# The second SwiGLU network in seven half-block products

## The chip, the cores and the metric

One core of one Trainium2 chip runs the kernel. The metric is the time of one execution on the device, in microseconds.

## What is computed

One layer of a decoder, on 1024 tokens and 16 learned ones ahead of them, in float32: a half-weighted SwiGLU network, two attentions mixed by gates, a second half-weighted SwiGLU network. The case is about the last one:

```python
def swiglu_ffn(u, w_gu, w_down):
    g, up = jnp.split(u @ w_gu, 2, axis=-1)
    return (jax.nn.silu(g) * up) @ w_down
...
        h = h + 0.5 * swiglu_ffn(rms_norm(h, ffn2_norm[l]), ffn2_w_gu[l], ffn2_w_down[l])
    return h[:, N_META:]
```

D_MODEL is 1024, D_FF is 2816; w_gu is 1024 x 5632, w_down 2816 x 1024.

## The kernel before

Tensors lie in blocks of 128 partitions: the model's width is KD = 8 blocks, the hidden width FT = 22. h stays on the chip, transposed (width on the partitions, tokens along the free axis). Every float32 product is made of three matmuls of fp32r operands (mm3, L71 to L75: high by high, low by high, high by low). ScalarE makes the high part (a cast), and VectorE or GpSimd the low part (the subtraction of the high part). So each 128 x 1024 block of weights that SP loads into `raw` costs ScalarE one cast (L387) and GpSimd one subtraction (L445).

ffn_phase computes both networks. For the second the tokens go in two chunks of 512 (REAL_TOKENS). It first normalizes: TensorE adds up the squares over the partitions (L199), ScalarE takes the root (L219), VectorE the reciprocal (L245), TensorE broadcasts it (L208), VectorE scales h (L252), and the two parts of u are made. Then there are 11 groups of two hidden blocks. gate_up multiplies the gate and up weights of a block with u, ScalarE applies silu (L411), VectorE multiplies (L523) and splits the hidden block (L526, L528); down multiplies the group before with its down weights, and VectorE adds half of each result to h (L539). The loops of TensorE, VectorE, ScalarE, GpSimd and SP over the groups are hardware loops (Fori). Each engine works through its own list in order, and waits on semaphores; SP issues every transfer in the order of its list, also one that waits for nothing, behind those that wait. The last group is followed by Store: TensorE transposes h back (L299), ScalarE and VectorE copy the rows (L312), and SP stores them (L319). The output projection (out_proj_phase) runs just before the second network; it is written out, without a loop.

## Time and profile before

| | us |
|---|---|
| median of 3 runs | 2772.76 |
| lowest and highest | 2771.84, 2775.6 |
| span of the profiled execution, first to last instruction | 2767.1 |
| first matmul of the second network's gate | 2033.05 |
| first transpose behind its last matmul | 2755.83 |

The profiled execution has no time of its own beside the span; the median of the runs lies 5.7 us above it. Busy time is the time in which an engine worked on an instruction. The columns behind the bar in a group give the idle time just before its instructions and what ended most of it. The granted clock is the share of TensorE's full speed (2.4 GHz) that it was given; 0.5 is 1.2 GHz.

### The profile page before, as it was taken

The numbers are of one execution on the slowest core, as the hardware profiler recorded it, in microseconds if no ns is written. First come the engines' busy times: TensorE is split into PE (matmuls) and PEld (weight loads), VectorE is DVE, ScalarE is ACT, GpSimd is POOL, SyncE is SP. The second block draws the span as 40 slices with busy tenths as digits, with TensorE's granted clock in tenths as the row PEclk, the third lists the DMA queues.
The fourth block names the chain that finished last, engine by engine and source line by source line (L and its number), as shares of the span: only waits on it lengthen the run. The fifth ranks groups of instructions, "written<-read, shape, count | busy, mean of one in ns | idle before, by whom it ended". The sixth has DMA issues, their size and how long they took to land. (4 is left out here: it accounts for less than half of the span.)

```text
span 2767.1 us, 37228 instructions
## 1 busy us (share of the span) xinstructions
PE 2600.7 (94%) x13802; PEld 2307.1 (83%) x13802; DVE 1106.3 (40%) x1994; ACT 682.5 (25%) x1285; POOL 749.7 (27%) x711
## 2 busy tenths in 40 slices
PE   7999999999978999988999979997979999999999
PEld 6999999999968888876787768886868888888887
DVE  5233332333375566533766651112143333333324
ACT  4111111111044445432444441112131111111101
POOL 4222222222122333221444462222142222222210
PEclk8999999999989999987988999999989999999999
DMA  3211111111011000000000011112021111111101
GB/s 127 67 47 46 47 46 47 46 47 46 8 76 47 25 24 0 1 31 9 4 7 4 3 39 61 45 38 92 31 68 61 46 58 49 45 45 45 51 33 61
DMA packets 32510, 116.05 MB, mean 42 GB/s; under 512 B 4016, under 2 KB 5936, under 8 KB 32256
## 3 DMA queue, kind: packets, MB, share of 16 engines
q1 hardware_dynamic: 32384, 114.29, 12.3%
q8 instruction: 89, 1.46, 0.2%
q14 instruction: 37, 0.30, 0.0%
HBM read 105.49 MB, written 8.65 MB: 41 GB/s over the span
## 5 line engine op out<-in xcount | busy, mean ns | idle before, releaser
L73 PE MATMUL f_bank<-u_hi,f_w_hi 128*128 128x384 f32 (+2 forms) x1760 | 612.5, 348 | 16.6 <-POOL u_lo L232 13.3
L445 POOL TENSOR_TENSOR f_w_lo<-f_raw,f_w_hi 128x1024 fp32r<-128x1024 f32 x132 | 328.2, 2507 | 1101.9 <-ACT f_w_hi L387 1101.9
L74 PE MATMUL f_bank<-u_hi,f_w_lo 128*128 128x384 f32 (+2 forms) x1760 | 611.9, 348 | 0.0
L75 PE MATMUL f_bank<-u_lo,f_w_hi 128*128 128x384 f32 (+2 forms) x1760 | 611.8, 348 | 0.0
L523 DVE TENSOR_TENSOR f_work<-f_work,f_bank 128x384 f32<-128x384 f32 (+2 forms) x110 | 64.3, 584 | 781.2 <-PE f_bank L75 771.0
L73 PEld LDWEIGHTS f_bank<-u_hi,f_w_hi 128*128 128x128 f32 x1760 | 332.3, 189 | 45.9 <-issue 18.3
L75 PEld LDWEIGHTS f_bank<-u_lo,f_w_hi 128*128 128x128 f32 x1760 | 332.1, 189 | 27.6
L74 PEld LDWEIGHTS f_bank<-u_hi,f_w_lo 128*128 128x128 f32 x1760 | 332.2, 189 | 27.5
L75 PE MATMUL f_bank<-f_hid_lo,f_w_hi 128*128 128x384 f32 (+2 forms) x880 | 306.3, 348 | 0.0
L74 PE MATMUL f_bank<-f_hid_hi,f_w_lo 128*128 128x384 f32 (+2 forms) x880 | 306.0, 348 | 0.0
L73 PE MATMUL f_bank<-f_hid_hi,f_w_hi 128*128 128x384 f32 (+2 forms) x880 | 305.7, 347 | 0.0
L387 ACT CAST f_w_hi<-f_raw 128x1024 fp32r<-128x1024 f32 x132 | 132.4, 1050 | 548.7 <-PE f_bank L75 537.7
L411 ACT ACTIVATE f_work<-f_bank 128x384 f32<-128x384 f32 (+2 forms) x110 | 56.6, 516 | 625.2 <-PE f_bank L75 625.2
L73 PEld LDWEIGHTS f_bank<-f_hid_hi,f_w_hi 128*128 128x128 f32 x880 | 165.8, 188 | 13.6
L75 PEld LDWEIGHTS f_bank<-f_hid_lo,f_w_hi 128*128 128x128 f32 x880 | 165.2, 188 | 13.7
L74 PEld LDWEIGHTS f_bank<-f_hid_hi,f_w_lo 128*128 128x128 f32 x880 | 165.2, 188 | 13.6
L539 DVE SCALAR_TENSOR_TENSOR h_in<-f_bank,h_in 128x384 f32<-128x384 f32 (+1 forms) x264 | 135.7, 518 | 98.6 <-PE f_bank L75 98.4
L539 DVE SCALAR_TENSOR_TENSOR h_out<-f_bank,h_out 128x512 f32<-128x512 f32 x176 | 119.1, 689 | 90.2 <-PE f_bank L75 90.2
L1510 POOL TENSOR_TENSOR mla_p_lo<-mla_p,mla_p_hi 128x512 fp32r<-128x512 f32 (+4 forms) x112 | 106.4, 950 | 67.7 <-DVE mla_p_hi L1861 67.5
L73 PE MATMUL fox_bank<-u_hi,fox_w_hi 128*128 128x384 f32 (+1 forms) x288 | 98.3, 341 | 16.5 <-DVE fox_w_lo L1267 16.5
L528 DVE TENSOR_TENSOR f_hid_lo<-f_work,f_hid_hi 128x384 fp32r<-128x384 f32 (+2 forms) x110 | 109.0, 991 | 3.8
L73 PE MATMUL gt_bank<-u_hi,gt_w_hi 128*128 128x512 f32 x256 | 100.7, 393 | 9.6 <-POOL gt_w_lo L1920 9.6
(277 smaller groups left out, 4287.1 us busy)
## 6 DMA issues: line engine op xcount, KB each, us to landing
f_raw<-in_ffn SPq DMA_DIRECT2D x132, 512.0 KB, 3.8
gt_raw<-in_gate SPq DMA_DIRECT2D x24, 512.0 KB, 3.7
fox_raw<-in_fox SPq DMA_DIRECT2D x12, 512.0 KB, 4.4
kept_hsave<-h_in SPq DMA_DIRECT2D x1, 4160.0 KB, 12.7
h_out<-kept_hsave SPq DMA_DIRECT2D x8, 520.0 KB, 6.3
ld_xin<-in_x SPq DMA_DIRECT2D x8, 512.0 KB, 4.5
op_raw<-in_wout SPq DMA_DIRECT2D x8, 512.0 KB, 5.4
out<-f_raw SPq DMA_DIRECT2D x6, 512.0 KB, 4.1
```

Source lines behind the costliest of these rows:

```text
L73: nc.tensor.matmul(out, w_hi, x_hi, start=first, stop=False)
L74: nc.tensor.matmul(out, w_lo, x_hi, start=False, stop=False)
L75: return nc.tensor.matmul(out, w_hi, x_lo, start=False, stop=last)
L387: nc.scalar.copy(w_hi[:, slot, :], raw[:, n_rem, :]).then_inc(whi_done, 1)
L411: nc.scalar.activation(silu[:, u % 2, 0:n], bank[2 * (u % 2)][:, 0:n], ACT.Silu).then_inc(silu_done, 1)
L445: nc.gpsimd.tensor_tensor(w_lo[:, slot, :], raw[:, raw_slot, :], w_hi[:, slot, :].bitcast(F32), ALU.subtract).then_inc(wlo_done, 1)
L523: nc.vector.tensor_tensor(h32[:, 0:n], silu[:, u % 2, 0:n], bank[2 * (u % 2) + 1][:, 0:n], ALU.mult).then_inc(h32_done, 1)
L528: nc.vector.tensor_tensor(hid_lo[:, parity, f, columns(t0, n)], h32[:, 0:n], hid_hi[:, parity, f, columns(t0, n)].bitcast(F32), ALU.subtra ...
L539: nc.vector.scalar_tensor_tensor(g.h[:, d, t0:t0 + n], bank[4 + v % 4][:, 0:n], 0.5, g.h[:, d, t0:t0 + n], ALU.mult, ALU.add).then_inc(dow ...
L1510: nc.gpsimd.tensor_tensor(p_lo[:, w % 2, 0:n], p32[:, w % 2, 0:n], p_hi[:, w % 2, 0:n].bitcast(F32), ALU.subtract).then_inc(plo_done, 1)
```

## The change

The first network keeps its code, under the name plain_ffn_phase. The second gets a new ffn_phase, written out without loops, with W = 512 tokens in each half.

It uses Strassen's form (Winograd's variant of it). Both large products are cut in two along tokens, inner width and outer width: seven products of half blocks stand for eight. For gate and up a group p (FP = 11 of them) is 2 gate and 2 up blocks, and each is cut into two halves of the inner width; 7 steps j = 0 to 6 each multiply a sum of weight quarters with a sum of input quarters (4 blocks of inner width, 2 halves x of output blocks: 24 matmuls of 512 columns). The results are added up in four pairs of PSUM banks where the form allows it; ScalarE copies intermediate sums out (snap), VectorE the last ones (evacuate). The seven sums of u (split into both parts) stay on the chip in u_hi, u_lo and two new tensors. For that, u's quarters are computed in place of h, which SP saves to DRAM first (save) and brings back later (reload). VectorE makes the four sums of weights per group (weight_mix) and all low parts (weight_lo, u_lo). GpSimd makes only the four sums of the down weights, which SP loads (load_down) and stores to DRAM in blocks of 128 columns, 512 bytes (store_down). The hidden blocks and their sums go to DRAM too (store_hidden, store_first, store_mixed).

Only after all 77 steps come the down products: 28 units n (7 products jj x 4 output blocks), each 11 x 3 matmuls; load_s brings the unit's weights (704 KB), load_t the hidden pieces (512 KB), ScalarE and VectorE split them (s_hi, s_lo, t_hi, t_lo), add_down adds to h. The transposes, copies and stores of the output lie among the last 12 units. The host rearranges the weights accordingly. The diff, cut:

```diff
-def ffn_phase(nc, g, tag, d_blocks, gain_col, chunks, first=False):
+def plain_ffn_phase(nc, g, tag, d_blocks, gain_col, chunks, first=False):
...
+FP = FT // 2
+STEPS = 7 * FP
+UNITS = 28
+SUM_OF = {1: (1, 2), 2: (None, 0), 3: (3, None), 4: (0, 1)}
+RAW_OF = {0: 0, 5: 3, 6: 2}
+TARGET = ((4, 1), (0, 1), (0, 0), (0, 0), (0, 1), (4, 1), (4, 0))
...
+def ffn_phase(nc, g, tag, d, gain_col, tb, W, first=False):
...
+        T1, T2, T3, T4 = [hf[:, n * W:(n + 1) * W] for n in range(4)]
+        WD = [hf[:, 4 * W + 512 * k:4 * W + 512 * k + 512] for k in range(4)]
...
+        def t_raw(z):
+            x = piece(z % 6)
+            return rw[:, 4 * D + (z % 3) * 2 * W:4 * D + (z % 3) * 2 * W + x.stop - x.start]
...
+        @block.sync
+        def _(sp):
+            def load(m):
+                sp.dma_start(raw_block(m), d["gu"][m // 4, m % 4]).then_inc(raw_in[m % 5], 16)
+            def save(i, kh, th):
...
+                sp.dma_start(d["keep"][x], g.h[x]).then_inc(h_saved[i], 16)
...
+            def store_first(p):
+                sp.wait_ge(t_done, 4 * p + 1)
+                sp.dma_start(d["hid"][0, :, p, :], T1).then_inc(t1_stored, 16)
...
+            def store_mixed(p):
+                sp.wait_ge(t_done, 4 * p + 4)
+                sp.dma_start(d["hid"][4:7, :, p, :].rearrange("j p w -> p j w"),
...
+            def load_down(i):
+                if i == 0:
+                    sp.wait_ge(blo_done, 14)
+                else:
+                    sp.wait_ge(s_stored, 64 * i)
+                sp.dma_start(hf[:, 4 * W:4 * W + 4 * 512], d["wd"][i]).then_inc(wd_in, 16)
+            def store_down(i):
+                sp.wait_ge(s_added, 4 * i + 4)
+                for k in range(4):
+                    sp.dma_start(d["dsum"][k, :, :, i * P:(i + 1) * P].rearrange("a p b -> p a b"),
+                                 WD[k].rearrange("p (a b) -> p a b", a=4)).then_inc(s_stored, 16)
+            def load_t(z):
+                jj, q = z // 6, z % 6
+                if z >= 3:
+                    sp.wait_ge(tlo_done, z - 2)
+                src = d["hid"][jj].rearrange("p a b -> p (a b)")[:, piece(q)]
+                sp.dma_start(t_raw(z), src).then_inc(rt_in[z % 3], 16)
...
+            def load_s(n):
+                if n >= 2:
+                    sp.wait_ge(slo_done, n - 1)
+                sp.dma_start(s_raw(n), s_source(n)).then_inc(rs_in[n % 2], 16)
+            def reload(i, tiles):
+                x = (slice(None), tiles, slice(tb, tb + 2 * W))
+                sp.dma_start(g.h[x], d["keep"][x]).then_inc(h_back[i], 16)
...
+            load(0)
+            save(0, 0, 0)
+            load(1)
+            load(2)
+            save(1, 0, 1)
+            save(2, 1, 1)
+            load(3)
+            load(4)
+            save(3, 1, 0)
+            for p in range(FP):
+                if p:
+                    store_hidden(p - 1)
+                    load_down(p - 1)
+                if p + 1 < FP:
+                    sp.wait_ge(add_done, 4 * p + 4)
+                    load(4 * p + 5)
+                    load(4 * p + 6)
+                if p:
+                    store_first(p - 1)
+                    store_mixed(p - 1)
+                    store_down(p - 1)
+                if p + 2 < FP:
+                    sp.wait_ge(wlo_done, 7 * p + 6)
+                    load(4 * p + 8)
+                if p + 1 < FP:
+                    sp.wait_ge(wlo_done, 7 * p + 7)
+                    load(4 * p + 7)
+            load_down(FP - 1)
+            sp.wait_ge(wlo_done, STEPS - 2)
+            sp.wait_ge(t1_stored, 16 * (FP - 1))
+            for z in range(3):
+                load_t(z)
+            store_down(FP - 1)
+            sp.wait_ge(b_stored[(FP - 2) % 2], 48 * (FP // 2))
+            sp.wait_ge(t_done, 4 * (FP - 1))
+            reload(0, slice(4, KD))
+            sp.wait_ge(add_done, 4 * FP)
+            sp.wait_ge(s_stored, 64 * FP)
+            load_s(0)
+            sp.wait_ge(wlo_done, STEPS)
+            load_s(1)
+            reload(1, slice(2, 4))
+            for z in range(3, 5):
+                load_t(z)
+            store_first(FP - 1)
+            sp.wait_ge(t1_stored, 16 * FP)
+            load_t(5)
+            store_hidden(FP - 1)
+            store_mixed(FP - 1)
+            sp.wait_ge(t_stored, 16 * FP)
...
+            for n in range(UNITS):
...
+                if n + 2 < UNITS:
+                    load_s(n + 2)
+                if jj < 6:
+                    for q in PIECES_OF[dp]:
+                        load_t(6 * (jj + 1) + q)
+                if not first and n >= 20:
...
+        @block.gpsimd
+        def _(pool):
+            for i in range(FP):
+                pool.wait_ge(wd_in, 16 * (i + 1))
+                nc.gpsimd.tensor_tensor(WD[3], WD[2], WD[3], ALU.add).then_inc(s_added, 1)
...
+            def t_hi(z):
+                jj, q = z // 6, z % 6
+                if z == 0:
...
+                nc.scalar.copy(t_buf(near_hi, far_hi, jj)[:, piece(q)], t_raw(z)).then_inc(thi_done, 1)
+            def s_hi(n):
+                if n >= UNITS:
+                    return
+                if n == 0:
+                    act.wait_ge(prod_done, 2 * (STEPS - 3))
...
+                act.wait_ge(rs_in[n % 2], 16 * (n // 2 + 1))
+                nc.scalar.copy(s_buf(near_hi, w_hi, n), s_raw(n)).then_inc(shi_done, 1)
...
+            for st in range(3, STEPS):
+                snap(st - 1, 1)
+                silu(st - 1, 1)
+                weight_hi(st + 2)
+                if st == STEPS - 3:
+                    t_hi(0)
+                    t_hi(1)
+                elif st == STEPS - 2:
+                    t_hi(2)
+                    t_hi(3)
+                elif st == STEPS - 1:
+                    t_hi(4)
+                    s_hi(0)
...
+            def product(st, x):
+                p, j = st // 7, st % 7
+                out = ps[(0, 2, 0, 2, 0, 2, 0)[j] + x]
+                if x == 0:
+                    pe.wait_ge(wlo_done, st + 1)
+                if j == 0 and p:
...
+                elif j == 6:
+                    pe.wait_ge(up_done, 2 * p + 1 + x)
...
+                for k in range(4):
+                    if p == 0 and x == 0 and k % 2 == 0:
+                        pe.wait_ge(blo_done, 2 * j + k // 2 + 1)
...
+                    for i, (w, u) in enumerate(((wh, uh), (wl, uh), (wh, ul))):
+                        for b in range(NS):
+                            last = nc.tensor.matmul(out[:, b, 0:N], w[:, c], u[:, b * N:(b + 1) * N],
+                                                    start=(j in (0, 1, 5) and k == 0 and i == 0),
+                                                    stop=(k == 3 and i == 2), skip_group_check=True)
+                last.then_inc(prod_done, 1)
+            def down(n):
...
+                pe.wait_ge(slo_done, n + 1)
+                if n < 2:
+                    pe.wait_ge(hid_done, 4 * FP - 1 + n)
...
+                for k in range(FP):
+                    if dp == 0 and k % 2 == 0:
+                        pe.wait_ge(tlo_done, 6 * jj + k // 2 + 1)
...
+            def evacuate(st, x):
+                p, j = st // 7, st % 7
...
+                dve.wait_ge(prod_done, 2 * st + x + 1)
+                if j == 3:
...
+                    nc.vector.tensor_tensor(parts(e2(p, x)), acc(2 + x), parts(e2(p, x)), ALU.add).then_inc(gate_done, 1)
+                elif j == 4:
+                    dve.wait_ge(snapped, 6 * p + 3 + x)
+                    nc.vector.tensor_tensor(parts(e5(p, x)), acc(x), parts(e5(p, x)), ALU.add).then_inc(up_done, 1)
+                    dve.wait_ge(up_done, 2 * p + 1 + x)
+                    dve.wait_ge(silu_done, 4 * p + 1 + x)
...
+            def first_sum(p):
+                dve.wait_ge(hid_done, 4 * p + 3)
...
+                nc.vector.tensor_tensor(T1, e2(p, 0), e1(p, 0), ALU.subtract).then_inc(t_done, 1)
...
+            def more_sums(p):
+                dve.wait_ge(hid_done, 4 * p + 4)
...
+            def t_lo(z):
+                jj, q = z // 6, z % 6
+                dve.wait_ge(thi_done, z + 1)
+                nc.vector.tensor_tensor(t_buf(near_lo, far_lo, jj)[:, piece(q)], t_raw(z),
...
+            def s_lo(n):
...
+                dve.wait_ge(shi_done, n + 1)
+                nc.vector.tensor_tensor(s_buf(near_lo, w_lo, n), s_raw(n), s_buf(near_hi, w_hi, n).bitcast(F32),
+                                        ALU.subtract).then_inc(slo_done, 1)
...
+            dve.wait_ge(rooted, 2 if first else 1)
+            if first:
+                nc.vector.reciprocal(rstd[0:META, 0:1], rstd[0:META, 0:1])
+            nc.vector.reciprocal(rstd[:, 1:QT + 1], rstd[:, 1:QT + 1]).then_inc(inverted, 1)
+            weight_lo(0)
+            scaled(0, 0)
+            u_lo(0, 0)
+            u_lo(0, 1)
+            weight_mix(1)
+            scaled(0, 1)
+            mix_first(0)
+            mix_first(1)
+            weight_lo(1)
+            scaled(1, 1)
+            u_lo(1, 0)
+            u_lo(1, 1)
+            mix_second(0)
+            mix_second(1)
+            weight_mix(2)
+            mix_third(0)
+            mix_third(1)
+            u_lo(2, 0)
+            u_lo(2, 1)
+            weight_lo(2)
+            weight_mix(3)
+            u_lo(3, 0)
+            u_lo(3, 1)
+            weight_lo(3)
+            weight_mix(4)
+            u_lo(4, 0)
+            u_lo(4, 1)
+            scaled(1, 0)
+            u_lo(5, 0)
+            u_lo(5, 1)
+            mix_fourth(0)
+            mix_fourth(1)
+            weight_lo(4)
...
+            for st in range(3, STEPS):
+                p, j = st // 7, st % 7
+                evacuate(st - 1, 1)
+                weight_lo(st + 2)
+                weight_mix(st + 3)
+                if p and j == 2:
+                    first_sum(p - 1)
+                if p and j == 3:
+                    more_sums(p - 1)
+                if st == STEPS - 3:
+                    t_lo(0)
+                    t_lo(1)
+                elif st == STEPS - 2:
+                    t_lo(2)
+                    t_lo(3)
+                elif st == STEPS - 1:
+                    t_lo(4)
+                    s_lo(0)
+                evacuate(st, 0)
+            first_sum(FP - 1)
+            evacuate(STEPS - 1, 1)
+            s_lo(1)
+            more_sums(FP - 1)
+            t_lo(5)
+            for n in range(UNITS):
+                add_down(n - 1)
...
@@ -2179,7 +2969,7 @@
             hb = placed(nc, stream, "")
             g.h, g.sumsq = hb("h_out", [P, KD, T]), hb("sumsq_out", [P, T])
             out_proj_phase(nc, g)
-            ffn_phase(nc, g, "f2", g.dram["ffn2"], g.FFN2_GAIN, REAL_TOKENS)
```

SUM_OF, RAW_OF, QUARTER_OF and TARGET say which sums a step takes and where a result is added. slot(w, st) gives three weight slots in turn; snap and silu on ScalarE follow TensorE by half a step. T1 to T4 and WD lie in the room of h. Before the loop of ScalarE stand weight_hi(0), the root, the copies of the broadcast, u_hi and weight_hi(1) to weight_hi(4), in the order of VectorE's list above.

## Rows read from the trace of the kernel before

**Rows 1.** The page: span, then busy time of each engine, its share and instructions.

```profile
span 2767.1 us, 37228 instructions
...
PE 2600.7 (94%) x13802; PEld 2307.1 (83%) x13802; DVE 1106.3 (40%) x1994; ACT 682.5 (25%) x1285; POOL 749.7 (27%) x711
```

**Rows 2.** Busy us (instructions) by stretch, engines as headed, then clock, DMA share, GB/s.

```profile
core 0: us, PE busy (x) PEld busy (x) DVE busy (x) ACT busy (x) POOL busy (x), PEclk, DMA share, GB/s
1925.00:1950.00 25.00, 25.00 (x112) 20.69 (x111) 2.85 (x5) 4.03 (x4) 5.46 (x3) 1.00 0.40 141
...
2033.00:2037.20 4.20, 4.16 (x10) 3.33 (x11) 4.20 (x5) 1.42 (x4) 3.97 (x2) 0.53 0.19 42
2045.00:2100.00 55.00, 55.00 (x244) 45.58 (x243) 13.57 (x15) 8.90 (x11) 17.35 (x7) 1.00 0.24 77
...
2600.00:2700.00 100.00, 100.00 (x443) 82.83 (x442) 28.09 (x38) 12.21 (x15) 19.91 (x8) 1.00 0.11 37
```

**Rows 3.** Groups by shape after 2000 us: busy, mean ns, idle before, releaser.

```profile
L73 PE MATMUL f_bank<-u_hi,f_w_hi 128*128 128x512 f32 x704 | 274.7, 390 | 8.0 <-POOL u_lo L232 8.0
...
L539 DVE SCALAR_TENSOR_TENSOR h_out<-f_bank,h_out 128x512 f32<-128x512 f32 x176 | 119.1, 689 | 90.2 <-PE f_bank L75 90.2
L528 DVE TENSOR_TENSOR f_hid_lo<-f_work,f_hid_hi 128x512 fp32r<-128x512 f32 x44 | 74.6, 1697 | 1.5
L387 ACT CAST f_w_hi<-f_raw 128x1024 fp32r<-128x1024 f32 x66 | 66.2, 1052 | 280.3 <-PE f_bank L75 276.0 <-DMA f_raw<-in_ffn 4.3
...
L411 ACT ACTIVATE f_work<-f_bank 128x512 f32<-128x512 f32 x44 | 26.3, 598 | 294.0 <-PE f_bank L75 294.0
```

**Rows 4.** In order of time, second network's start: start, us, engine, line.

```profile
2017.07 1.28 SPq L363 DMA_DIRECT2D f_raw<-in_ffn  x3
2017.09 1.28 ACT L219 ACT_TABLE_LOAD   x1 [1.79 <-PEq L2049]
...
2017.13 3.55 PE L199 MATMUL f_bank<-ones,sumsq_out 128*128 128x1 f32 x16 [7.50 <-PEq L2049]
2020.71 0.27 ACT L219 ACTIVATE f_norm_rstd<-f_bank,gains 128x8 f32<-128x8 f32 x1 [2.34 <-PE f_bank L199]
...
2021.27 3.78 PE L208 MATMUL f_bank<-ident,f_norm_rstd 128*128 128x128 f32 x16 [0.60 <-DVE f_norm_rstd L245]
...
2033.05 0.76 PE L73 MATMUL f_bank<-u_hi,f_w_hi 128*128 128x512 f32 x1 [7.99 <-POOL u_lo L232]
```

**Rows 5.** In order of time at the end, TensorE.

```profile
2755.83 4.82 PE L299 MATMUL f_bank<-ident,h_out 128*128 128x128 f32 x40
```

**Rows 6.** Groups by shape over the whole span, VectorE: busy us, mean ns.

```profile
L1267 DVE TENSOR_TENSOR fox_w_lo<-fox_raw,fox_w_hi 128x512 fp32r<-128x512 f32 x24 | 16.1, 682 | 4.3 <-ACT fox_w_hi L1003 4.3
...
L252 DVE SCALAR_TENSOR_TENSOR f_work<-h_out,gains,f_bank 128x512 f32<-128x512 f32 x16 | 11.2, 741 | 2.2 <-PE f_bank L208 2.2
...
L2035 DVE TENSOR_TENSOR gt_o_lo<-o_mla,gt_o_hi 128x1024 fp32r<-128x1024 f32 x2 | 6.8, 3417 | 0.0
...
L821 DVE TENSOR_TENSOR lt_w_lo<-lt_raw,lt_w_hi 128x1024 fp32r<-128x1024 f32 x1 | 1.2, 1226 | 6.1 <-ACT lt_w_hi L799 6.1
```

**Rows 7.** The same groups, GpSimd.

```profile
L993 POOL TENSOR_TENSOR fox_p_lo<-fox_p,fox_p_hi 128x512 fp32r<-128x512 f32 x36 | 46.4, 1294 | 39.7 <-DVE fox_p_hi L1351 39.7
```

**Rows 8.** DMA issues over the span: KB each, median us to landing.

```profile
f_raw<-in_ffn SPq DMA_DIRECT2D x132, 512.0 KB, 3.8
...
kept_hsave<-h_in SPq DMA_DIRECT2D x1, 4160.0 KB, 12.7
...
mla_w_head<-in_mla SPq DMA_DIRECT2D x8, 192.0 KB, 2.4
...
ident<-in_ident SPq DMA_DIRECT2D x1, 64.0 KB, 1.8
```

**Rows 9.** GB/s in 40 equal slices of the stretch 1905 to 1960 us.

```profile
GB/s 0 0 0 0 0 0 45 370 407 407 398 425 388 378 367 354 352 380 311 30 0 0 0 0 244 428 97 0 0 12 0 12 277 404 76 0 0 0 0 0
```

**Rows 10.** In order of time at the end, VectorE.

```profile
2760.69 0.69 DVE L312 COPY f_raw<-f_bank 128x512 f32<-128x512 f32 x1 [0.18 <-PE f_bank L299]
```

488 lines of the change are left out of this document (484 added, 4 removed).

## The prediction

> **What bounds the kernel now.** I read the page first. TensorE is busy 94% of the 2767.1 us span; VectorE has 40%, ScalarE 25%, GpSimd 27% [rows 1]. The chain of work that ended last also lies on TensorE. The windows then say how evenly it runs: in the second network (from 2033 us) TensorE has no idle time, the granted clock is 1.00 (the 2.4 GHz level), and 443 matmuls start in 100 us, 226 ns each [rows 2]. The groups by shape confirm the cover: VectorE waits 90.2 us for TensorE before the additions at L539 and ScalarE 276.0 us before L387, never the other way round except for 8.0 us at the start (L73 waits for u_lo) [rows 3]. So a matmul taken away is worth its 226 ns, as long as what prepares and empties it keeps up.
>
> **What the change takes away.** Gate, up and down are 44 x 8 + 22 x 8 = 528 blocks of 128 x 128 weights, each times two token chunks and three split terms: 3168 matmuls of 512 columns. Their phase begins at 2033.05 [rows 4] and ends at 2755.83 [rows 5]. Ten of them ran at clock 0.53 (the 1.2 GHz level) in 4.2 us [rows 2], 1.9 us more than at 226 ns; 24 transposes of 4.82/40 = 0.12 us, 2.8 us, lie among them. That leaves (2755.83 - 2033.05 - 1.9 - 2.8)/3168 = 0.2267 us each. After the change there are 77 steps x 2 x 4 x 3 = 1848 and 28 units x 11 x 3 = 924, in all 2772, again of 512 columns: 628.4 us, where 718.2 were. The 396 matmuls are worth **89.8 us**. A step is then 5.44 us and a down unit 7.48 us. That all of it is unrolled costs nothing: the unrolled output projection also starts 112 matmuls in 25 us, beside 141 GB/s [rows 2].
>
> **Steady steps.** Per seven steps (38.1 us) VectorE has 11 operations of 1024 elements at 1.226 us and 14 of 512 at about 0.69 [rows 3, 6]: 23.1 us. ScalarE has 7 x 1.05 + 10 x 0.6 = 13.4 us [rows 3]. GpSimd adds 4 x 1.3 us [rows 7]. All fit. The tightest hand-over is the last product of a group of seven to the first of the next, through one pair of banks: 0.69 us of emptying against 2.7 us of the other half's product. GpSimd can lengthen it: a subtraction beside a GpSimd one took 1.70 us (L528) [rows 3] where 0.68 us is the time alone (L1267) [rows 6]; two engines alternating made 1.2 us into 3.4 (L2035) [rows 6]. Even 4 x 1.3 us added gives 28.3 of 38.1 us, so I take nothing, with 2.6 us per group as the other end. SBUF — State Buffer in the Trainium skill (Who interferes with whom) says that the second of the two engines blocks fully until the first is done; the rows agree, and by that rule the worst case is the 2.6 us, which the rival below prices.
>
> **Start, +17.1 us.** Before, TensorE starts 12 us after the broadcast begins and then never waits. Now VectorE alone prepares seven sums of the input. ScalarE splits a weight block before it takes the root: a load takes 3.8 us to land [rows 8], so the root comes at 2017.07 + 3.8 + 1.05 + 1.28 (a table load, L219 [rows 4]) = 2023.2 instead of 2020.7; then 0.3 + 0.3 + 2.1 for the first broadcast + 0.6 for its copy: the first scaling at 2026.4. The stored copy of h has landed by then (1.5 MB at some 390 GB/s [rows 9] and 2 us of landing: 2024). From there to the fifth step VectorE has 16 scalings of 0.70 (0.69 of L539 and 0.74 of L252 [rows 3, 6]), 12 low parts, 8 mixes of the input, 4 mixes and 4 low parts of weights: 11.2 + 28 x 1.226 = 45.5 us. TensorE can't do step 5 before 2071.9; it has done four steps (21.8 us) by then, so it is as if it had started at 2050.1. After each gap the clock falls; the last one costs about 2 us more, as above: 2052.1, against 2033.05 + 1.9 = 2035.0. First matmul near 2030.5, gaps of some 5, 4 and 6 us before steps 2, 3 and 5. Bounds: 11 us if the root isn't delayed and the hand-overs cost nothing, 24 us if each of some 40 hand-overs costs 0.15 us more.
>
> **From products to down units, +38.3 us.** This is what the order of SP's queue makes. Let t = 0 be the start of step 73 (j = 3 of the last group). The three sums of group 9 end at 1.7 (ScalarE's split) + 1.2 + 2.1 = 5.0. Behind them SP stores 0.79 MB and the four mixed down blocks, 1.05 MB in pieces of 512 bytes. Saturated transfers run at 354 to 428 GB/s [rows 9] (I take 390) and a landing costs some 2 us besides (512 KB 3.8, 4160 KB 12.7 [rows 8]). The trace has no such store. By bytes it takes 2.7 us. If nothing of the 128 pieces in the identity matrix's 1.8 us overlapped [rows 8], its 2048 pieces would take 29. 64 KB and 192 KB, each 128 pieces, differ by 0.6 us [rows 8], so the bytes count and the pieces little; I take 4.5 us, near the low end. s_stored comes at 5.4 + 2.0 + 4.5 + 2 = 14. Only then SP loads the last down weights (4.7 us, 18.7) and, behind them, the first three hidden pieces, the first at about 20. But VectorE stands at t_lo(0), in step 74, and behind that at evacuate(74, 0), for which product 76 waits: it starts at about 24 instead of 16.3. Next GpSimd adds until 24, the store and a 2.1 MB reload of h occupy the queue until 34.5, load_s(0), load_s(1), 1.05 MB and load_t(3) follow: 3.7 + 2.7 + 1.3, landing at 44.2. VectorE stands at t_lo(3) before evacuate(75, 0). From there t_hi and t_lo 2.3, two evacuations 1.4, t_lo(4) about 3 with ScalarE's silus and splits, s_lo(0) 1.9, evacuate(76, 0) 0.7: down(0) starts at 53.5. Without stalls it would start at 4 x 5.44 = 21.8: **31.8 us**. Then load_s(2) queues behind store_mixed(10) and reload(2): its s_lo is ready 20 us after down(0) starts, two units need 15: 5 us. The clock after these gaps 1.5 us. Bounds: 28 us (store by bytes alone, nothing lost in hand-overs) to 50 us.
> DMA: Bandwidth & Descriptors in the Trainium skill (Specifications) puts line rate at pieces of 512 bytes or more. No row here shows it. By it the store takes 2.7 us and this term is 3.6 us smaller, about 2735 us in the end.
>
> **Down units.** In 7.48 us VectorE has 1.7 + 1.8 + 0.7 + 0.7 = 4.9 us and the queue moves 1.5 MB, 200 GB/s of 390; a load is asked for two units ahead. Nothing.
>
> **End.** Now 40 transposes, a copy and a store stand behind the last matmul: 2767.1 - 2755.8 = 11.3 us [rows 5, 10]. After: addition 0.8, 4 transposes 0.5, two copies 1.4, the last store of 256 KB 4.8: 7.5 us. The other 56 transposes lie among the units, 6.7 us.
>
> **The sum.** 2052.1 + 628.4 + 38.3 + 6.7 + 7.5 = 2733.0 of span against 2767.1: 34.1 us less. The median of the runs shown is 2772.8, 5.7 us above the span (launch and end around it), and I keep that: **2739 us**. The working's own bounds are -6 and +7 at the start and -10 and +12 in the middle; combined, 2722 to 2757.
>
> **Rivals.** First, the middle is covered better than I read it (the loads land before VectorE reaches them, or the stores drain in time): 30 us come back, 2709 us. For it: only the order of instructions, not their durations, says that VectorE stands still. Against: s_stored stands in front of the loads in the text of the change, and the sums that feed it end only in step 73. Chance 0.08.
> Second, GpSimd's additions fall on the tight hand-over in each group: 2.6 us x 11 = 29 us, 2767 us. For: the 1.70 and 3.4 us above. Against: the additions start early in a group, when there is slack. Chance 0.12.
> Third, slower than before: the stores in 512-byte pieces clog the queue in every group. The last load of a group is asked behind them; it lands at 28.7 us + s of a group, and VectorE needs it at about 41. From s = 12.3 us each further us costs 10 us over the groups, besides 2 in the middle: at s = 14 the gain is gone, at s = 20 it is +77 + 31 - 34 = 74 us, 2847 us. For: the 29 us bound. Against: the small difference of the two loads above. Chance 0.08.
> That the products aren't fewer can't be: the loops give 2772.
>
> **The numbers.** Forecast 2739 us, 0.72; the rivals 0.08, 0.12, 0.08. The range leaves out the first and the third and reaches to the second: 2716 to 2766. A measurement here can tell about 0.2%, 5.5 us: faster than 2767.2 has nearly all of the forecast, the first rival and a little under half of the second, 0.85; within 0.2% 0.06; slower 0.09.
>
> **What would show it.** 2772 matmuls of 512 columns at 0.227 us and clock 1.00 in the steady part; VectorE without pause before step 5; idle TensorE in three gaps at the start; then 8 us before product 76 and some 24 before down(0), VectorE idle before t_lo(0), t_lo(3) and s_lo(0) with a DMA as releaser; the store of mixed down blocks landing in about 6.5 us; under 1 us of idle TensorE per group between. I am wrong if TensorE idles in every group, if that store takes over 12 us, or if the two transitions together cost under 40 or over 75 us.

## The result, and the profile after

The changed kernel takes **2738.6 us** (median of 4 runs, 2737.0 to 2754.1) beside 2772.3 us for the kernel before on the same chip: a ratio of 0.9895, interval 0.9864 to 0.9925. It is 1.1% faster, and the forecast was 2739 us. A second measurement of the same file, the first experiment below, gives 0.9852 (0.9808 to 0.9895). The forecast was right in the time; several of its terms were off, with opposite signs.

The page of the kernel after, span and busy times (the lines that answer to [rows 1]):

```profile
span 2735.2 us, 36205 instructions
...
PE 2530.9 (93%) x13406; PEld 2242.9 (82%) x13406; DVE 1257.3 (46%) x2073; ACT 812.9 (30%) x1432; POOL 651.9 (24%) x681
```

TensorE's share has fallen from 94% to 93% although it is busy 69.8 us less: it waits now in places where it didn't. To compare only what the change touches, I measure each trace from SP's first load of the second network to the end of the span and call that **the stretch**. Before it is 2767.1 - 2017.07 = 750.0 us [rows 1, 4]; after it is 2735.2 - 2023.10 = 712.1 us. The prediction's terms, added up without what lies ahead, make 715.9. Steps are counted from 1 where the text speaks of the start, as the prediction does, and from 0 in names such as product 76 and down(0).

First, the groups that answer to [rows 3], after 2000 us (busy us, mean ns | idle before, releaser):

```profile
L1020 PE MATMUL f_ps<-u_hi,f_w_hi 128*128 128x512 f32 x352 | 140.9, 400 | 9.9 <-DVE u_lo L1117 6.7 <-DVE f_w_lo L1180 2.8
...
L1020 PE MATMUL f_ps<-f_far_hi,f_w_hi 128*128 128x512 f32 x264 | 104.3, 395 | 11.2 <-DVE f_ev L1193 7.2 <-DVE f_w_lo L1180 4.0
...
L1043 PE MATMUL f_ps<-u_hi,f_w_hi 128*128 128x512 f32 x110 | 43.3, 394 | 1.2 <-DVE f_w_lo L1234 1.2
...
L1043 PE MATMUL f_ps<-u_hi 128*128 128x512 f32 x66 | 27.3, 414 | 20.6 <-DVE u_lo L1234 20.6
```

Line 1020 is the seven products, line 1043 the down units. The idle time ahead of them is most of what the change gives back: 13.5 us of waiting for VectorE's low parts at the start (6.7 + 2.8 + 4.0), 7.2 us for an emptied bank at L1193, 20.6 us for the first hidden pieces of the down units and 1.2 us for the weights of the third unit. Second, three windows (columns as in [rows 2]): the steady steps, the transition and the down units.

```profile
2300.00:2400.00 100.00, 99.92 (x440) 82.22 (x439) 64.26 (x69) 33.36 (x44) 16.86 (x9) 1.00 0.48 163
2480.00:2510.00 30.00, 8.97 (x28) 7.05 (x29) 11.37 (x14) 5.74 (x6) 0.76 (x1) 0.61 0.61 227
2600.00:2700.00 100.00, 100.00 (x459) 82.94 (x458) 51.37 (x48) 35.59 (x35) 0.00 (x0) 1.00 0.57 188
```

In the steady steps 440 matmuls start in 100 us, against 443 before: a little is missing. In the transition TensorE works 9 of 30 us while the DMA engines are 0.61 busy and VectorE 11.4 us. Among the down units it has no idle time.

The start, TensorE, in order of time (start, us, engine, line; in brackets the idle time before and what ended it). The first row is the broadcast of the root, and each further one ends a gap:

```profile
2030.50 3.79 PE L1069 MATMUL f_ps<-ident,ssum 128*128 128x128 f32 x16 [3.81 <-DVE ssum L1273]
2037.32 0.76 PE L1020 MATMUL f_ps<-u_hi,f_w_hi 128*128 128x512 f32 x1 [3.04 <-DVE u_lo L1117]
2049.50 0.47 PE L1020 MATMUL f_ps<-u_hi,f_w_hi 128*128 128x512 f32 x1 [3.65 <-DVE u_lo L1117]
2059.63 0.51 PE L1020 MATMUL f_ps<-u_hi,f_w_hi 128*128 128x512 f32 x1 [2.83 <-DVE f_w_lo L1180]
...
2076.46 0.47 PE L1020 MATMUL f_ps<-f_far_hi,f_w_hi 128*128 128x512 f32 x1 [4.01 <-DVE f_w_lo L1180]
```

Three gaps after the first matmul, before steps 2, 3 and 5, as predicted, with 3.7, 2.8 and 4.0 us where I had 5, 4 and 6. The transition, SP's queue first and ScalarE and VectorE behind it:

```profile
2462.10 3.96 SPq L732 DMA_DIRECT2D kept_dsum<-h_out  x4
2468.85 0.35 SPq L727 DMA_DIRECT2D h_out<-in_wd  x1
2469.30 1.60 SPq L740 DMA_DIRECT2D f_rw<-kept_hid  x3
2480.78 3.34 SPq L732 DMA_DIRECT2D kept_dsum<-h_out  x4
2484.23 0.51 SPq L749 DMA_DIRECT2D h_out<-kept_keep  x1
2486.92 0.83 SPq L745 DMA_DIRECT2D f_rw<-kept_dsum  x2
2487.80 0.44 SPq L749 DMA_DIRECT2D h_out<-kept_keep  x1
2488.28 0.95 SPq L740 DMA_DIRECT2D f_rw<-kept_hid  x2
```

```profile
2475.04 1.04 ACT L890 CAST u_hi<-f_rw 128x1024 fp32r<-128x1024 f32 x1 [10.36 <-DMA f_rw<-kept_hid]
...
2499.55 1.04 ACT L890 CAST u_hi<-f_rw 128x1024 fp32r<-128x1024 f32 x1 [20.99 <-DMA f_rw<-kept_hid]
```

```profile
2476.11 3.52 DVE L1226 TENSOR_TENSOR u_lo<-f_rw,u_hi 128x1024 fp32r<-128x1024 f32 x2 [10.18 <-ACT u_hi L890]
2479.56 0.68 DVE L1193 TENSOR_TENSOR f_ev<-f_ps,f_ev 128x512 f32<-128x512 f32 x1
...
2500.63 1.23 DVE L1226 TENSOR_TENSOR u_lo<-f_rw,u_hi 128x1024 fp32r<-128x1024 f32 x1 [16.85 <-ACT u_hi L890]
```

The store of the mixed down blocks is issued at 2462.10; the last down weights can be asked for only when it has landed, at 2468.85; the first hidden pieces follow, and ScalarE has waited 10.4 us for them when it starts at 2475.04. VectorE's low part starts at 2476.11, and the emptying (L1193) for which product 76 waits stands behind it in the list. The same happens again with the fourth piece: 21.0 us on ScalarE, 16.9 on VectorE, 20.6 on TensorE. Here it is also the bytes queued ahead of the piece that take the time, for the DMA engines are busy throughout (columns as in [rows 2]):

```profile
2487.00:2499.00 12.00, 0.63 (x3) 0.19 (x1) 0.00 (x0) 0.00 (x0) 0.00 (x0) 0.64 1.02 415
```

### The profile page after: what moved, and what is told of

Read it like the earlier page. It is cut to its first block and busy times, and to the rows that moved or that the text cites. A ratio compares the mean times of both kernels' runs of the same rounds, so it can differ in the third digit from the quotient of the medians.

```text
span 2735.2 us, 36205 instructions
## 1 busy us (share of the span) xinstructions
PE 2530.9 (93%) x13406; PEld 2242.9 (82%) x13406; DVE 1257.3 (46%) x2073; ACT 812.9 (30%) x1432; POOL 651.9 (24%) x681
## 5 line engine op out<-in xcount | busy, mean ns | idle before, releaser
L73 PE MATMUL f_bank<-u_hi,f_w_hi 128*128 128x384 f32 (+1 forms) x1056 | 338.4, 320 | 8.7 <-POOL u_lo L232 5.1
L75 PE MATMUL f_bank<-u_lo,f_w_hi 128*128 128x384 f32 (+1 forms) x1056 | 338.0, 320 | 0.0
L74 PE MATMUL f_bank<-u_hi,f_w_lo 128*128 128x384 f32 (+1 forms) x1056 | 338.0, 320 | 0.0
L445 POOL TENSOR_TENSOR f_w_lo<-f_raw,f_w_hi 128x1024 fp32r<-128x1024 f32 x66 | 162.3, 2477 | 566.7 <-ACT f_w_hi L387 566.6
L75 PE MATMUL f_bank<-f_hid_lo,f_w_hi 128*128 128x272 f32 (+1 forms) x528 | 169.5, 321 | 0.0
L74 PE MATMUL f_bank<-f_hid_hi,f_w_lo 128*128 128x272 f32 (+1 forms) x528 | 169.2, 321 | 0.0
L73 PE MATMUL f_bank<-f_hid_hi,f_w_hi 128*128 128x272 f32 (+1 forms) x528 | 168.8, 320 | 0.0
L1020 PE MATMUL f_ps<-u_hi,f_w_hi 128*128 128x512 f32 x352 | 140.9, 400 | 9.9 <-DVE u_lo L1117 6.7
L1020 PE MATMUL f_ps<-u_hi,f_w_lo 128*128 128x512 f32 x352 | 139.6, 397 | 0.0
L1020 PE MATMUL f_ps<-u_lo,f_w_hi 128*128 128x512 f32 x352 | 139.5, 396 | 0.0
```

The lines of the kernel that those rows point to most:

```text
L73: nc.tensor.matmul(out, w_hi, x_hi, start=first, stop=False)
L74: nc.tensor.matmul(out, w_lo, x_hi, start=False, stop=False)
L75: return nc.tensor.matmul(out, w_hi, x_lo, start=False, stop=last)
L445: nc.gpsimd.tensor_tensor(w_lo[:, slot, :], raw[:, raw_slot, :], w_hi[:, slot, :].bitcast(F32), ALU.subtract).then_inc(wlo_done, 1)
L1020: last = nc.tensor.matmul(out[:, b, 0:N], w[:, c], u[:, b * N:(b + 1) * N], start=(j in (0, 1, 5) and k == 0 and i == 0), stop=(k == 3 and ...
```

## The experiments

All spans are compared by the stretch, since what lies ahead of it wanders (below). Ratios are against the kernel before on the same chip. c1 repeats the changed kernel beside the first experiments, e6 edits the kernel before, all others edit the changed one.

**c1, the same file again.**

> The changed kernel once more, unedited, as the mark for the others of this call. My theory: the stretch from SP's first load of the second network to the end takes 712 us again (2023.1 to 2735.2 before), while the stages ahead of it, which the change doesn't touch, move by some us with the granted clock in the attention (2023.1 was 6 us later than in the kernel before). Median 2732 to 2740. Rival: the new phase itself disturbs the stages ahead of it (their code lies elsewhere in memory); then its start is at 2023 again, to within 1 us.

2735.99 us, ratio 0.9852 (0.9808 to 0.9895); stretch 2740.2 - 2026.88 = 713.3 us, gaps of 7.1 and 20.5 us in the transition. So the stretch repeats within 1.2 us. Its start doesn't: over the eleven kernels of this section it lies between 2015.4 and 2028.1 us though the code ahead of it is the same in all. The expectation's rival, the start at 2023 again, falls; its theory, the clock in the attention, no run here shows.

**e6, the matmuls by themselves.** The kernel before, with the same 396 matmuls fewer and nothing of Strassen's form; the gate product leaves out two of its eight blocks and the up product one, so both are computed only in part.

```diff
-                            for k in range(KD):
+                            K = KD if square_sum else (KD - 2 if which == 0 else KD - 1)
+                            for k in range(K):
```

> The kernel BEFORE with 396 matmuls left out of the second network and nothing else changed: the gate product leaves out two of its 8 blocks of inner width, the up product one, so part of both products is missing. It has the 2772 matmuls of the changed kernel without any of its sums, stores and reloads. My theory: 396 x 0.2267 = 89.8 us less than before, 2683 us (2680 to 2686), since TensorE alone sets that phase; the 34 us gained are then 89.8 less about 56 lost at the start and in the middle. Rival: other engines take over as the bound when TensorE does less, and under 80 us are gained.

2681.09 us, ratio 0.9671 (0.9633 to 0.9708). The stretch is 2679.6 - 2019.20 = 660.4 us, 89.6 less than before, where 89.8 were predicted. A window of this kernel shows that nothing else became the bound:

```profile
2200.00:2300.00 100.00, 100.00 (x442) 82.87 (x442) 41.55 (x51) 14.20 (x17) 25.58 (x10) 1.00 0.16 53
```

So the change is worth 89.6 us of matmuls and pays back 712.1 - 660.4 = 51.7 us. By the terms of the table below, some 15 of them are lost at the start (33.3 us, where it was 17.9 before), 3 between the groups and 34 from the products to the down units, and the end returns 1. The rest of this section is on these 51.7.

**e1, the hidden pieces earlier.** Theory: product 76 waits because its emptying stands in VectorE's list behind t_lo(0), whose load SP issues behind the store of the mixed down blocks. Rival: it waits for the bank or for the sums themselves. The three loads and their waits move ahead of that store:

```diff
                     store_first(p - 1)
+                    if p == FP - 1:
+                        sp.wait_ge(wlo_done, STEPS - 2)
+                        sp.wait_ge(t1_stored, 16 * (FP - 1))
+                        for z in range(3):
+                            load_t(z)
                     store_mixed(p - 1)
...
-            sp.wait_ge(wlo_done, STEPS - 2)
-            sp.wait_ge(t1_stored, 16 * (FP - 1))
-            for z in range(3):
-                load_t(z)
```

> One edit in SP's list: the first three hidden pieces are asked for before the stores of group 9 (behind store_first), not behind load_down of the last group. My theory is that down(0) is set by the chain store of mixed down blocks, s_stored, last down weights, GpSimd, store, s_stored, load_s(0) and load_t(3), and that product 76 only waits for the first pieces. So the 7.2 us gap before product 76 goes to under 1.5 us, the gap before down(0) grows from 20.7 to 27 to 31 us, and the time stays (-1 to +4 us on the changed kernel). Rival: the two gaps are independent, each with its own cause; then the time falls by 6 to 8 us.

2738.73 us, ratio 0.9877 (0.984 to 0.9914), stretch 712.5 us. TensorE's waits in the transition (us in total, times, longest):

```profile
PE f_ps L1044 <- DVE u_lo L1235: 30.0, 1, 30.0
PE f_ps L1044 <- DVE f_w_lo L1235: 1.4, 1, 1.4
```

The gap before product 76 is gone and the one before down(0) has grown from 20.6 to 30.0 us. That bears the theory out for the first gap. It also shows that this gap isn't additional time: the end of the transition is set by a later transfer (ScalarE waits 32.4 us for the fourth piece here, 21.0 in the changed kernel), and what TensorE gets earlier it waits for afterwards.

**e2, a product first that needs nothing of the last group.** If the order of SP's queue makes the transition, another order of the same work should take it away; if the bytes do, it should not. Of the down products the one with the raw block of weights is taken first, its pieces are loaded ahead of the stores of the last group, and the reloads of h and the stores come afterwards. The core of the edit:

```diff
-TARGET = ((4, 1), (0, 1), (0, 0), (0, 0), (0, 1), (4, 1), (4, 0))
+ORDER = (2, 0, 1, 3, 4, 5, 6)
+TARGET = ((0, 0), (4, 1), (0, 1), (0, 0), (0, 1), (4, 1), (4, 0))
...
-            jj, dp = n // 4, n % 4
+            jj, dp = ORDER[n // 4], n % 4
...
-                src = d["hid"][jj].rearrange("p a b -> p (a b)")[:, piece(q)]
+                src = d["hid"][ORDER[jj]].rearrange("p a b -> p (a b)")[:, piece(q)]
...
                     store_first(p - 1)
+                    if p == FP - 1:
+                        sp.wait_ge(wlo_done, STEPS - 2)
...
+                        for z in range(3):
+                            load_t(z)
                     store_mixed(p - 1)
                     store_down(p - 1)
...
+            load_t(3)
+            load_t(4)
+            sp.wait_ge(add_done, 4 * FP)
+            load_s(0)
             load_down(FP - 1)
...
```

> The down products in another order: product 2, whose weights need no sum, comes first, and SP asks for pieces, weights 0 to 3 and the last group's hidden blocks ahead of the last store of mixed down blocks, which nothing needs for 30 us then. The same arithmetic. My theory (both gaps are waits for transfers that stand behind s_stored in SP's list): both gaps go, at most 3 us of idle TensorE are left between product 75 and unit 1, the time falls by 24 to 30 us on the changed kernel, to some 2711 us. Rival 1: VectorE's own splitting work between step 74 and down(0) (8 operations, about 12 us) is the limit; then under 15 us come back. Rival 2: the transfers merely collide later, and a wait of over 8 us appears in units 2 to 8.

2708.51 us, ratio 0.9769 (0.973 to 0.9808); stretch 2702.2 - 2016.53 = 685.7 us, **26.4 less**. What is left of the waits:

```profile
PE f_ps L1049 <- DVE u_lo L1232: 2.1, 1, 2.1
PE f_ps L1049 <- DVE u_lo L1240: 1.6, 1, 1.6
PE f_ps L1049 <- DVE f_far_lo L1232: 1.4, 1, 1.4
```

29.0 us of idle time (7.2 + 20.6 + 1.2) have become 5.1, with the same loads and stores, and no longer wait appears in the units that follow. So it isn't the number of bytes by itself that costs the time: the order puts them ahead of what TensorE needs next. The expectation's other rival, VectorE's own splitting as the limit, falls too.

**e3 and e3b, the stores of mixed down blocks made larger.** This is the prediction's third rival by itself: each mixed block is stored four times (e3b: twice), into tensors of its own, and s_stored counts accordingly.

```diff
+REPEAT = ("dsum", "spare_a", "spare_b", "spare_c")
...
-                for k in range(4):
-                    sp.dma_start(d["dsum"][k, :, :, i * P:(i + 1) * P].rearrange("a p b -> p a b"),
-                                 WD[k].rearrange("p (a b) -> p a b", a=4)).then_inc(s_stored, 16)
+                for name in REPEAT:
+                    for k in range(4):
+                        sp.dma_start(d[name][k, :, :, i * P:(i + 1) * P].rearrange("a p b -> p a b"),
+                                     WD[k].rearrange("p (a b) -> p a b", a=4)).then_inc(s_stored, 16)
```

> Each store of the mixed down blocks is made four times (three into spare tensors), in the same pieces of 512 bytes. To be read in the stretch from SP's first load of the second network to the end, 713 us in the changed kernel. In the changed kernel one store takes about 4 us of SP's and the queue's time. My theory, the third rival's sum: four take 16 to 17 us, beyond the 12.3 us that a group has to spare; so TensorE idles some 4 us in each of 10 groups, and 2 x 12 us come on top in the chain at the end: +60 to +70 us, TensorE waiting for VectorE's weight low parts behind a DMA. Rival: the groups have more room than I worked out (loads of the next group overtake, or VectorE catches up); then only the chain's +24 us.

> The same with two stores instead of four: 8 us, under the 12.3 us to spare. My theory: no idle TensorE in the groups, only the chain at the end grows, by 2 x 4 us: the stretch takes 721 us instead of 713. Rival: any additional transfer in a group costs; then +40 us and more.

e3 took 2764.55 us (one run, beside 2770.63 for the kernel before), its stretch 734.7 us: +22.6, not the +60 to 70 of my theory. e3b took 2739.64 (one run), stretch 719.8: +7.7. In e3 each set of stores occupies SP for about 15 us, more than the 12.3 from which the prediction had let the groups suffer. Yet ten groups lose nothing. The waits in 2110 to 2440 us and the window 2120 to 2440 of e3, then that window after:

```profile
DVE f_rw L1170 <- DMA f_rw<-in_gu: 30.3, 8, 4.5
...
2120.00:2440.00 320.00, 319.69 (x1402) 262.25 (x1401) 199.97 (x213) 107.45 (x141) 52.31 (x32) 1.00 0.74 240
```

```profile
2120.00:2440.00 320.00, 319.69 (x1402) 262.41 (x1400) 206.50 (x212) 106.55 (x140) 60.84 (x32) 1.00 0.45 156
```

The late load does make VectorE wait, 8 times up to 4.5 us. But the sums it makes there are for a step three ahead, and TensorE starts 1402 matmuls in 320 us either way. My threshold took "when VectorE needs it" for "when TensorE needs what VectorE makes of it". All of the 22.6 us are in the transition (18.4 before product 76, 30.7 before down(0), 2.2 behind), where no slack is left.

**e4, the same store in large pieces.** dsum written in pieces of 2048 bytes instead of 512, at the same size; the blocks then lie otherwise than they are read, so the down weights are wrong.

```diff
-                    sp.dma_start(d["dsum"][k, :, :, i * P:(i + 1) * P].rearrange("a p b -> p a b"),
-                                 WD[k].rearrange("p (a b) -> p a b", a=4)).then_inc(s_stored, 16)
+                    sp.dma_start(d["dsum"][k].rearrange("a p b -> (a p b)")[i * P * 512:(i + 1) * P * 512].rearrange(
+                                     "(p b) -> p b", p=P), WD[k]).then_inc(s_stored, 16)
```

> The mixed down blocks are stored in pieces of 2048 bytes in place of 512, as many bytes; their layout in DRAM is then not what load_s expects, so the down products use wrong weights. My theory: issue and transfer of a store fall from 6.7 us (first issue to landing) to about 4.7, and the chain at the end has two of them: the stretch takes 3 to 4.5 us less than 713. Rival (the line-rate rule of the Trainium skill, DMA: Bandwidth & Descriptors, Specifications: 512 bytes suffice): less than 1 us.

2729.5 us (one run), stretch 2727.7 - 2015.40 = 712.3: no difference. My theory of 3 to 4.5 us less was wrong. The gaps are 6.8 and 21.2 us instead of 7.2 and 20.6. The prediction had charged the small pieces 1.8 us over the bytes; they cost nothing that shows in the stretch. The trace has a small difference, which the path doesn't keep: from the first issue of the store to the next load it is 6.40 us instead of 6.75, the second time 5.05 instead of 6.14, but from the issue of this second store to ScalarE's start on the fourth piece it is 19.4 us instead of 18.8. DMA: Bandwidth & Descriptors in the Trainium skill (Specifications) puts line rate at pieces of 512 bytes or more, and by that rule the two forms cost the same, as their stretches do here. What the trace shows beside the bytes is SP's own time, nearly 1 us for each of the four DMAs (3.96 us above), a little less with large pieces (3.40).

**e5, the root before the weights.** The start by itself: ScalarE takes the root before it splits the first block of weights.

```diff
-            weight_hi(0)
             if not first:
                 act.wait_ge(summed, 1)
...
+            weight_hi(0)
             for th in range(2):
                 act.wait_ge(bc_ready, th + 1)
```

> One edit in ScalarE's list: the first weight block is split behind the root, not ahead of it. In the changed kernel the root starts 6.8 us after SP's first load and the first scaling 10.2 us after. My theory: the root starts at 3.6 us, and since VectorE is the bound from there on, everything behind it comes 3.0 to 3.3 us earlier: 709.6 us for the stretch. Rival: the stored copy of h is late then, and the first or second scaling waits for its landing; under 1.5 us are gained. Too small for the median (2 to 3 us of 2738); to be read in the trace.

2730.23 us, ratio 0.9832 (0.9803 to 0.9861); stretch 2733.5 - 2024.42 = 709.1, 3.0 less than after and 4.2 less than c1. The root starts 3.6 us after SP's first load instead of 6.8, the first scaling at 7.0 instead of 10.2, step 5 at 50.2 instead of 53.4. What is late next shows in its own row: the first scaling waits 0.57 us for the stored copy of h.

```profile
2031.44 2.74 DVE L1112 SCALAR_TENSOR_TENSOR h_out<-h_out,gains,sumsq_out 128x512 f32<-128x512 f32 x4 [0.57 <-DMA kept_keep<-h_out]
```

**e7, the first weight sums on GpSimd.** VectorE is the bound of the start, so one may want to give GpSimd four of its sums. Theory 1: step 5 comes earlier by their time. Theory 2: beside GpSimd VectorE's own operations become longer and nothing is won.

```diff
+            nc.gpsimd.tensor_tensor(mix_block(1), A21, A22, ALU.add).then_inc(add_done, 1)
...
-            weight_mix(1)
...
-            weight_mix(2)
...
-            weight_mix(3)
...
-            weight_mix(4)
```

> The first four weight sums move from VectorE to GpSimd, which is idle at the start; the same arithmetic. At the start VectorE is the bound (step 5 begins 53.2 us after SP's first load). Theory 1: the two engines work side by side; VectorE has 4 x 1.18 = 4.7 us less to do, and step 5 begins 4 to 5 us earlier. Theory 2, as the 3.4 us of the 1024-element subtractions at L2035 say: one of the two waits while the other has two inputs in SBUF; a GpSimd sum of 1024 elements takes 2.4 us and VectorE stands meanwhile, so step 5 begins 0 to 5 us LATER. I hold with theory 2.

2739.62 us (one run), stretch 716.5: +4.4. Step 5 starts at 57.1 instead of 53.4. GpSimd and VectorE of this kernel, start and duration:

```profile
2031.71 2.60 POOL L830 TENSOR_TENSOR f_rw<-f_rw 128x1024 f32<-128x1024 f32 x1 [33.16 <-DMA f_rw<-in_gu]
2034.45 2.61 POOL L833 TENSOR_TENSOR f_rw<-f_rw 128x1024 f32<-128x1024 f32 x1
```

```profile
2031.35 6.91 DVE L1126 SCALAR_TENSOR_TENSOR h_out<-h_out,gains,sumsq_out 128x512 f32<-128x512 f32 x4 [1.76 <-ACT sumsq_out L951]
...
2040.52 2.73 DVE L1126 SCALAR_TENSOR_TENSOR h_out<-h_out,gains,sumsq_out 128x512 f32<-128x512 f32 x4
```

Four scalings take 6.91 us while GpSimd makes two sums, 2.73 us alone. SBUF — State Buffer in the Trainium skill (Who interferes with whom) lets the second engine stand until the first is done; the excess of 4.2 us, of the 5.2 us that the two sums take, agrees. It goes both ways: GpSimd's last sum takes 7.79 us (from 2061.78) beside VectorE's low parts, which keep their 2.35 us a pair. Over its three sets of scalings beside GpSimd VectorE takes 8.4 us more, and it is rid of four sums, some 4.6 us; that leaves the 3.7 us by which step 5 is late.

**e8, e2 and e5 together.**

> The raw product first (26.4 us less in the stretch, as measured) together with the root first. My theory: the two add up, the start and the middle have nothing in common: the stretch takes 682.5 us (681 to 684), the median 2700 to 2708. Rival: with an earlier start the transfers in the middle are late by as much; then as the raw product first alone, 685.7 us.

2706.68 us, ratio 0.9758 (0.9731 to 0.9785); stretch 2700.6 - 2016.94 = 683.7, where the two gains added give 682.7. They lie at different places and add, within the 1.2 us by which a stretch repeats.

**e9, e8 with one operation later.** The steady steps of all these kernels lack 3 matmuls in 100 us. TensorE at the first matmul of a group, and VectorE's list at the same time, in the changed kernel:

```profile
2132.67 0.39 PE L1020 MATMUL f_ps<-f_far_lo,f_w_hi 128*128 128x512 f32 x1
2133.10 0.47 PE L1020 MATMUL f_ps<-u_hi,f_w_hi 128*128 128x512 f32 x1
2133.41 0.40 PE L1020 MATMUL f_ps<-u_hi,f_w_lo 128*128 128x512 f32 x1
```

```profile
2131.13 1.22 DVE L1163 TENSOR_TENSOR f_rw<-f_rw 128x1024 f32<-128x1024 f32 x1
2132.27 1.52 DVE L1202 TENSOR_TENSOR h_out<-f_ps,h_out 128x512 f32<-128x512 f32 x2
```

Starts are 0.43 and 0.31 us apart instead of 0.227 twice: 0.29 us lost, in each of ten groups from 2094.70 to 2440.30. The bank is emptied at L1202, whose first operation ends about 2132.96, behind a sum of weights (L1163) that nobody needs yet; the matmul was due at 2132.90. The edit puts the emptying first:

```diff
                 weight_lo(st + 2)
-                weight_mix(st + 3)
+                if j != 6:
+                    weight_mix(st + 3)
...
                 evacuate(st, 0)
+                if j == 6:
+                    weight_mix(st + 3)
```

> On top of the two edits: in the last step of each group of seven VectorE empties the first bank pair (evacuate) before it makes the next weight sum, not after it. In the traces TensorE pauses about 0.3 us at the first matmul of every group (starts 0.43 and 0.31 us apart instead of 0.227), and VectorE's emptying ends 0.14 us before it. My theory: VectorE's list order is the cause; the pauses go, 10 x 0.3 = 3 us less than the 683.7 us of both edits, 680.7 us (680 to 682). Rival: the pause belongs to the turn of the code or to the restart of the banks, not to VectorE: then the pauses stay.

2699.23 us, ratio 0.9733 (0.9707 to 0.9758); stretch 679.5, 4.2 less than e8 where 3.0 were expected. 3.4 of them are there when product 76 starts; the others lie in the transition, whose waits are 5.3 us in all instead of 7.2, which no run here explains. All of these pauses are gone:

```profile
2100.00:2200.00 100.00, 100.00 (x443) 82.87 (x442) 64.53 (x67) 34.38 (x46) 19.30 (x11) 1.00 0.48 163
```

With 443 matmuls in 100 us the steady steps are at the pace of the kernel before [rows 2]. The timed intervals of e8 and e9 overlap; the trace is what tells them apart. e9 is the fastest version here, 2.7% below the kernel before where the change alone is 1.1% below.

## Why the prediction was right, point by point

| term | predicted | measured |
|---|---|---|
| matmuls taken away | 89.8 | 89.6 (e6) |
| start, as if TensorE then never waited | 35.0 | 33.3 |
| 2772 matmuls | 628.4 | 628.4 (no other pace in rows) |
| lost between groups | 0 | 3.0 |
| products to down units | 38.3 | 34.2 |
| transposes among the units | 6.7 | 6.4 |
| behind the last matmul | 7.5 | 6.6 |
| sum | 715.9 | 711.9 (the stretch is 712.1) |

**The matmuls.** The count and the price held; e6 shows it without anything else of the change. The step from busy share to value (a matmul taken away is worth its 226 ns) is the one on which the sign rested.

**The start.** The mechanism held: VectorE without pause, three gaps. Measured, the first matmul of the second group starts at 2094.70, 71.6 us into the stretch; less seven steps of 5.44 us and the 0.2 us of its own pause that is 33.3, where I had 35.0. The root came 0.7 us later than I had it (6.8 us after SP's first load), and the work behind it, from the first scaling to step 5, took 43.2 us instead of 45.5: pairs of 1024-element operations take 2.36 to 2.42 us, not 2 x 1.226, the single operation of [rows 6] being the one that I had taken, and single ones start 1.14 us apart. e5 confirms that the order on ScalarE, named in the prediction, costs 3 us.

**The groups.** I had the hand-over right ("the last product of a group of seven to the first of the next") and its cost wrong. I compared 0.69 us of emptying with 2.7 us of product and took nothing; what I left out is that the emptying is queued behind a weight split and a sum of 1.2 us each in VectorE's list. That the order is the cause is shown by e9. The other end, GpSimd at 2.6 us per group, doesn't occur: the second rival falls, as 319.7 of 320 us busy in the window above show. GpSimd and VectorE do lengthen each other in the groups, but away from the hand-over, where there is slack: VectorE's last sum of weights in a group (L1172) takes 2.0 us on average, the one before (L1168) 1.2, and GpSimd's four sums take 7.4 us a group where I had 5.2.

```profile
L1172 DVE TENSOR_TENSOR f_rw<-f_rw 128x1024 f32<-128x1024 f32 x11 | 22.1, 2012 | 0.0
...
L1168 DVE TENSOR_TENSOR f_rw<-f_rw 128x1024 f32<-128x1024 f32 x11 | 13.4, 1218 | 0.0
```

**The middle.** The order of SP's queue as the cause held (e1, e2), and the gaps came where they were named (7.2 and 20.6 us for 8 and 24). The sum was 4.1 us too large, in two terms. The delay up to down(0), 31.8 us, measured 29.8 (2508.28, where step 73 starts at 2456.74 and four steps take 21.8). What comes behind it, 5 us for load_s(2) and 1.5 of clock, measured 4.4: 1.2 us of waiting and some 3 of clock, since 14 matmuls behind the gap start 0.43 us apart. The weights of the third unit were ready about when I had them, 19.2 us after down(0) where I had 20; the slow matmuls made the two units before it take 18 us instead of 15. Behind the first gap the clock costs another 1.6 us, so it costs 4.7 us in all where I had 1.5, and part of that stands in the 29.8. The store came out nearly right, 6.75 us from its first issue to the next load where I had 6.5, but by another sum: I had 4.5 us of transfer and 2 of landing, and the trace shows 3.96 us in which SP issues the four DMAs, for which I had taken nothing, and 2.8 us behind them.

**The first rival** (the loads land in time) didn't happen in the changed kernel, but e2 is that case made: 685.7 us of stretch, 26.4 less, where I had priced it at 30.

**The third rival** had a wrong threshold. It said that the groups would suffer from 12.3 us of store; e3 has some 15 us of SP's time for each set and they don't. The slack of three steps ahead of TensorE was the missing term. Its price in the middle, 2 us for each us of store, stands if the us are those of SP's issue: e3b's further set, about 3.7 us, costs 7.7, and e3's three, 11 us, cost 22.6. Both are single runs, read in their traces.

**What lies outside the stretch.** The span is 2735.2 us where 2733.0 were predicted, and two errors cancel in it: the stretch is 3.8 us shorter, and it begins 6.0 us later than in the profile of before. The code ahead is the same. Its start lies at 2017.07 before, at 2019.20 in e6, and at 2015.4 to 2028.1 in the others; the difference already stands at the first load of the gate stage, 1635.6 before and 1641.1 after, 1634.7 in e8. No run here was made to say more of it, and I only call it spread between executions. The last 5.7 us, which I called launch and end around the span, were mostly something else: the profiled execution after took 2736.97 us, 1.8 more than its span, and the others 1.7 to 1.9. The rest is spread of the median against one execution, 1.6 us after, so that the median lies 3.4 us above the span and not 5.7. Together: -3.8 in the stretch, +6.0 ahead of it, -2.3 outside make -0.1 of 2738.7.

**The end.** 6.6 us where I had 7.5, though eight transposes stand behind the last down matmul and not four, as I had it.

Thus the time was met to half a us, and that near a hit is luck: the same file took 2736.0 us in c1. The working is right to about 6 us only, well inside the range of 2716 to 2766.

## What to carry to other kernels

An added step is queued twice: by what it needs, and by where it stands in the list of its engine. Compare each emptying of a bank with everything listed ahead of it, not with its own duration, and each load with the stores and waits ahead of it on SP; here 33 of the 52 us that the change gave back were such places (712.1 to 679.5 us in e9), and moving some lines returned them. A late transfer costs only what TensorE needs of it: follow it to the matmul before giving it a price, and at a transition, where no slack is left, expect time that is added on the path (e3, e3b), while time saved at one place may only become a wait at the next (e1, e4). And when two executions are compared, measure from a point behind which the code differs, or the spread of the rest stands in the term.

## What the runs showed of the hardware

- A matmul that starts 0.2 us late loses about 0.29: the next one also starts 0.31 us after it instead of 0.227 (ten times in the changed kernel, where the matmul is due at 2132.90 and starts at 2133.10; none in e9).
- SP issues a single DMA in 0.32 to 0.37 us, but back to back they take longer: 1.60 us for three loads of hidden pieces, 3.96 for four stores in pieces of 512 bytes, 3.40 for the same stores in pieces of 2048. So the size of the pieces is the smaller part of it; whether the rest is the issuing itself or a full queue, the runs don't separate.
- A GpSimd sum of 1024 elements takes 2.6 us; VectorE's four scalings beside two of them take 6.9 us instead of 2.7, and another such sum took 7.8 us (e7).
- Loads saturate at some 415 GB/s on this one core: 12 us in the transition, DMA share 1.02.
- From 0.45 to 0.74 of DMA share and from 156 to 240 GB/s (e3) TensorE's pace doesn't change: 1402 matmuls in 320 us in both.
- In gaps of 3 to 20 us the granted clock falls: 0.61 over the window 2480 to 2510, and 14 matmuls behind the gap of 20.6 us start 0.43 us apart, the pace of the 1.2 GHz level. Behind the gap of 2.8 us at the start, too, matmuls from 2060.49 on start 0.43 us apart.
